# High and low weight parts kept in DRAM by the first token pass of a feed-forward stage and loaded by the second

## The chip, the cores and the metric

The kernel runs on one core of a Trainium2 chip. The metric is the device time of one execution in microseconds; the median of three runs is given for the kernel before, and a profiled execution has a span (first to last instruction) and a time of its own.

## What is computed

One layer of a diffusion backbone on 1,152 tokens (1,024 latent, 128 context) with 1,024 channels: adaptive RMSNorm, an input projection, three mixers, an output projection and a residual; then a second norm and a SwiGLU feed-forward stage, which is what matters here:

```python
h2 = _rmsnorm(x, p['norm2_g'][l]) * (1.0 + sc2) + sh2
f = (jax.nn.silu(h2 @ p['ffn_w1'][l]) * (h2 @ p['ffn_w3'][l])) @ p['ffn_w2'][l]
return x + g2 * f
```

`ffn_w1` and `ffn_w3` are 1024 x 2816, `ffn_w2` is 2816 x 1024, all fp32; a final RMSNorm follows.

## The kernel before

Each fp32 operand is split into a high part (a cast to fp32r, made by ScalarE, ACT) and a low part (the operand less its high part, a subtraction by GpSimd, POOL, or VectorE, DVE). `three` (lines 785 to 789) then makes a product with three matmuls, high by high, high by low and low by high, on TensorE (PE).

The feed-forward stage takes the tokens in two passes (`ph` 0 and 1): 640 tokens, then 512, in halves of 320 and 256 (`HN`). In each pass a loop runs over the 2816 hidden columns, in 22 tiles of 128, two tiles (f = 0, 1) to a pair: 11 pairs (`NFB`) per pass, numbered p = 0 to 21. For one tile, `up` (L1132) computes both h2 @ w1 and h2 @ w3 by a scheme of Strassen's kind: seven products (x = 0 to 6) of weight blocks of 512 rows by 128 columns instead of eight, 12 matmuls each. Four of the weight blocks are sums and differences of the quarters of [w1, w3]. `down` (L1164) multiplies the gated result of a pair with two tiles of w2 and adds it to `acc`.

For every tile of both passes:
- SyncE (SP) loads w1 and w3 columns into `raw13[f]` (`w13_in`, L522 to 527, two transfers of 512 KB with rows of 512 bytes) and, per pair, two tiles of w2 into `f2s` (`w2_in`, L529 to 533). SP issues in the order of its program and waits in that order.
- VectorE makes the four sums: `w_sum_13` (L2013, L2015) and `w_sum_24` (L2022, L2024).
- ScalarE makes seven high parts, 128x512 each, `w13_high` (L1523), into `w13h[x]`. There is one `w13h` buffer for each x, used by both tiles of a pair, so a new high part waits for the product x of the tile before.
- GpSimd makes the low parts of x = 0, 1, 3, 4, 6 (`w13_lo`, shown as L744) and VectorE those of x = 2 and 5 (L2029). They are written in place over the raw block or its sum.
- The low and high parts of w2 are made by `w2_lo` on GpSimd (L748) and `w2_high` on ScalarE (L1527).

The seven products go to four PSUM banks (`BANK_OF`), so block x=5 waits until VectorE has added up x=3 from bank 3 (`sum_3`, L2043), and x=6 and the next tile wait in the same way. VectorE's `sum_2` (L2037), `sum_3` (L2043, L2045, L2048), `gated_first`, `gated_second`, `f_low` (L2074) and `gather` (L2083) turn the products into the gated rows and add the down products to `acc`. ScalarE's `first_product`, `gate_a`, `gate_b` and `f_high` take part.

The order of the work on each engine is the order written out in `pair_first` (first tile of a pair) and `pair_second` (second tile and `down`), one pair of functions for ScalarE and one for VectorE; `pair_lows` is GpSimd's. In the second pass VectorE also does the end of the tokens already finished, one piece per pair (`early` and `late`): `gate_sum` (L2201) and `end_add` (L2205), 128x1024 additions, and `end_scale`; `early` stands ahead of `sum_2` of the second tile. SP loads the saved residual (`last_x2`, L558) and stores results (`result_out`, L563).

Of `up`, the waits of each block:

```python
if x == 4:
    pe.wait_ge(sem("gated_act"), cnt(6, pr, 3 * f + 1))
if x >= 5:
    pe.wait_ge(sem("combined"), cnt(18, pr, 9 * f + 2 * x - 8))
if x in POOL_LO:
    pe.wait_ge(sem("w13_lo"), cnt(10, pr, 5 * f + POOL_LO.index(x) + 1))
else:
    pe.wait_ge(sem("w13_lo_dve"), cnt(4, pr, 2 * f + DVE_LO.index(x) + 1))
```

Of the kernel before, what the change touches and what calls it, by code (L numbers as in the profile page):

```python
# [53 lines left out]
POOL_LO, DVE_LO = (0, 1, 3, 4, 6), (2, 5)  # L54
HID_POOL, HID_DVE = ((6,), (4, 6)), ((0, 1, 2, 3, 5, 4), (0, 2, 1, 3, 5))
# [35 lines left out]
def build(nc, A, O):  # L91
# [161 lines left out]
    def w13_low(x, f, dt=F32R):  # L253
# [32 lines left out]
    kb_dram = nc.dram_tensor("kb_dram", [32, NPAIR, 15 * HD], F32).ap()  # L286
    x2_dram = nc.dram_tensor("x2_dram", [T, D], F32).ap()
# [60 lines left out]
    def _(sp):  # L348
# [173 lines left out]
        def w13_in(pr, f, tile, first=False):  # L522

            if not first:
                sp.wait_ge(sem("product"), cnt(2 * NPR, pr, NPR * f - NPR))
            for e, w in enumerate(UP):
                sp.dma_start(raw13[f][:, e, :, :], A[w][0].rearrange("(k p) n -> p k n", p=P)[:, :, bass.ds(tile * P, P)]).then_inc(sem(f"x{3 + f}_in"), 16)
# [37 lines left out]
        def pair_in(ph, pr, tile, following, first=False):  # L565

            if not first:
                for f in range(FB):
                    w2_in(ph, pr, f, tile + f)
            w13_in((pr[0], pr[1] + 1), 0, following)  # L570
            w13_in((pr[0], pr[1] + 1), 1, following + 1)

        pair_in(0, (0, 0), 0, 2, True)
        with sp.Fori(1, NFB - 1) as it:
            pair_in(0, (it, 0), 2 * it, 2 * it + 2)
        pair_in(0, (0, NFB - 1), 2 * NFB - 2, 0)
        for p in range(NFB, 2 * NFB - 1):
            t = 2 * (p - NFB)
            pair_in(1, (0, p), t, t + 2)
# [12 lines left out]
        for f in range(FB):  # L592
            w2_in(1, (0, 2 * NFB - 1), f, 2 * NFB - 2 + f)
        for i in range(5, 8):
            result_out(i)
# [6 lines left out]
    def _(pool):  # L602
# [138 lines left out]
        def w13_lo(pr, f, x):  # L741
            pool.wait_ge(sem("w13_hi"), cnt(2 * NPR, pr, NPR * f + x + 1))
            pool.wait_ge(sem("w_sums"), cnt(8, pr, 4 * f + 4))
# [6 lines left out]
        def pair_lows(ph, pr, turn=False, last=False):  # L750

            after = (pr[0], pr[1] + 1)
            for x in POOL_LO:
                w13_lo(pr, 1, x)
            for f in range(FB):
                w2_lo(pr, f)
            if turn:
                for x in HID_POOL[1]:
                    hid_low(1, x)
            if not last:  # L760
                for x in POOL_LO:
                    w13_lo(after, 0, x)

        for x in (0, 1, 3, 4):
            w13_lo((0, 0), 0, x)
        hid_low(0, 6)
        w13_lo((0, 0), 0, 6)
# [24 lines left out]
    def _(pe):  # L792
# [339 lines left out]
        def up(ph, pr, f, first=False, turn=False, late=False):  # L1132

            n = HN[ph]
            for x in range(NPR):
# [11 lines left out]
                if x in POOL_LO:  # L1147
# [9 lines left out]
                wlo = w13_low(x, f)  # L1157
# [51 lines left out]
    def _(act):  # L1209
# [378 lines left out]
        for x in (0, 1):  # L1588
            w13_high(zero, 0, x, True)
# [3 lines left out]
        for x in (2, 3):  # L1593
            w13_high(zero, 0, x, True)
# [3 lines left out]
        for x in (4, 5):  # L1598
            w13_high(zero, 0, x, True)
        act.wait_ge(sem("o_done"), 2 * NT + 1)  # L1600
        w13_high(zero, 0, 6, True)
        h2_norm(NT - 1)
        gate_a(0, zero, 0)
        for x in range(6):
            w13_high(zero, 1, x)
# [4 lines left out]
        w13_high(zero, 1, 6)  # L1610
# [4 lines left out]
        def pair_first(ph, pr):  # L1615

            first_product(ph, pr, 0)
            for x in range(4):
                w13_high(pr, 1, x)
            gate_a(ph, pr, 0)  # L1620
            for x in (4, 5):
                w13_high(pr, 1, x)
            f_high(ph, pr, 0, 0)
            w13_high(pr, 1, 6)
# [3 lines left out]
        def pair_second(ph, pr, first=False, turn=False, last=False):  # L1628

            first_product(ph, pr, 1)  # L1630
            for f in range(FB):
                w2_high(ph, pr, f)
# [7 lines left out]
            if not last:  # L1640
                for x in range(NPR):
                    w13_high((pr[0], pr[1] + 1), 0, x)
# [44 lines left out]
    def _(dve):  # L1687
# [427 lines left out]
        w13_lo(zero, 0, 2)  # L2115
# [4 lines left out]
        w13_lo(zero, 0, 5)  # L2120
# [5 lines left out]
        w13_lo(zero, 1, 2)  # L2126
# [4 lines left out]
        w13_lo(zero, 1, 5)  # L2131
        f_low(0, zero, 0, 1)

        def pair_first(ph, pr, turn=False, late=False):

            if not late:
# [4 lines left out]
            if late:  # L2141
                w_sum_13(pr, 1)
                sum_3(ph, pr, 0)
            w_sum_24(pr, 1)
            if not late:
                sum_3(ph, pr, 0)
            w13_lo(pr, 1, 2)
# [3 lines left out]
            w13_lo(pr, 1, 5)  # L2151
            f_low(ph, pr, 0, 1)

        def pair_second(ph, pr, first=False, turn=False, early=None, late=None, gated=0):
# [19 lines left out]
            else:  # L2174
# [6 lines left out]
            if turn:  # L2181
                w_sum_13(after, 0)
                hid_low(1, 2)
            w_sum_24(after, 0)
            if late:
                late[0](late[1])
            for c in range(4, 2 * len(FT[ph])):
# [3 lines left out]
                if c == (7 if turn else 4):  # L2191
                    w13_lo(after, 0, 2)
                if c == 6 and not turn:
                    w13_lo(after, 0, 5)
            if turn:
                hid_low(1, 3)
                w13_lo(after, 0, 5)
# [35 lines left out]
        pair_first(1, (0, NFB), turn=True, late=True)  # L2233
# [11 lines left out]
        pair_first(1, last, late=True)  # L2245
# [93 lines left out]
```

## Time and profile before

| | |
|---|---|
| median of 3 runs | 1374.13 us (1367.06 to 1375.0) |
| profiled execution, its time | 1372.36 us |
| its span | 1370.5 us |
| PE busy | 1236.8 us (90%) |
| DVE busy | 1001.0 us (73%) |
| POOL busy | 645.8 us (47%) |
| ACT busy | 565.2 us (41%) |
| moved by DMA | 164.69 MB, 120 GB/s over the span |

The profile is of one execution. Busy is the time in which an engine had an instruction in flight; matmuls are pipelined and their ends are modelled, so PE's durations overlap. A row of a timeline gives start, duration, engine, line, what is written and read, and in brackets the idle time before and what ended it. The first pass runs from about 538 to 973 us of the span, the second from 973 to 1358; a pair begins where SP issues its `f2s` loads.

### The profile page before, as it was taken

The page shows a single profiled execution, that of the slowest core. Times are in us where ns is not written, and L with a number is a line of the kernel's source. Part 1 is how long each engine was busy: PE and PEld are TensorE (multiplying, and loading weights), DVE is VectorE, ACT ScalarE, POOL GpSimd, SP SyncE. Part 2 cuts the span into 40 slices and gives each one's busy share as a digit, 9 for nine tenths or more (in the row PEclk, how much of TensorE's full clock was granted, in tenths as well). Part 3 has the DMA queues.
Part 4 walks back from the last instruction along what each step waited for, and adds up shares of the span by engine and source line. Part 5 has one row for each costly group of instructions (what it writes and reads, how often), then busy time and mean ns, then how long its engine had stood idle before and what let it go on. Part 6 is the DMA issues. An engine that isn't in the chain of part 4 may idle for free.

```text
span 1370.5 us, 21592 instructions
## 1 busy us (share of the span) xinstructions
PE 1236.8 (90%) x7574; PEld 1089.7 (80%) x7574; DVE 1001.0 (73%) x1470; ACT 565.2 (41%) x1021; POOL 645.8 (47%) x426
## 2 busy tenths in 40 slices
PE   6786888995699999899999999999999999999986
PEld 4386787895446888799999999998788888888875
DVE  5437459949954347666667766667999899888988
ACT  2642531117245546543333333343443444344333
POOL 0495105275243003544554444544676666566662
PEclk9888998897799999999999999999999999999998
DMA  8814145379872323233223123222232333333331
GB/s 313 304 69 152 39 145 169 92 84 220 269 291 92 123 93 123 63 92 92 67 86 92 62 91 92 62 91 64 90 124 92 108 122 123 107 107 123 107 108 62
DMA packets 149089, 164.69 MB, mean 120 GB/s; under 512 B 7342, under 2 KB 124376, under 8 KB 146344
## 3 DMA queue, kind: packets, MB, share of 16 engines
q1 hardware_dynamic: 147664, 159.23, 37.5%
q0 software_dynamic: 1280, 4.72, 0.9%
q8 instruction: 30, 0.49, 0.1%
q14 instruction: 27, 0.22, 0.1%
q10 hardware_dynamic: 88, 0.02, 0.0%
HBM read 140.35 MB, written 23.59 MB: 120 GB/s over the span
## 4 chain that ended last, share of the span: by engine, by line
PE 62%; DVE 12%; issue 9%; ACT 6%; POOL 4%; DMA 4%; SPq 3%; DVEq 0%; ACTq 0%; POOLq 0%
PE banks L787 18%; PE banks L788 17%; PE banks L789 17%; PE banks L1056 2%; ACT w13h L1523 1%; DVE acc L2205 1%; DVE raw13r L2029 1%; DVE acc L2083 1%; DVE wsums L2022 1%; DMA ad<-in_ada_w 1%; PE banks L872 1%; SPq L483 1%; PE banks L823 1%; DMA y_dram<-yb 1%; SPq L425 1%
## 5 line engine op out<-in xcount | busy, mean ns | idle before, releaser
L744 POOL TENSOR_TENSOR raw13r<-raw13s,w13h 128x512 fp32r<-128x512 f32 x132 | 199.1, 1518 | 391.0 <-DVE wsums L2024 277.3
L788 PE MATMUL banks<-ntr,w13h 128*128 128x256 f32 (+1 forms) x1144 | 338.2, 296 | 0.0
L787 PE MATMUL banks<-ntr,w13h 128*128 128x256 f32 (+1 forms) x968 | 286.8, 296 | 32.9 <-DVE u L2043 25.2
L788 PEld LDWEIGHTS banks<-ntr,w13h 128*128 128x128 f32 x1144 | 217.3, 190 | 0.9
L787 PEld LDWEIGHTS banks<-ntr,w13h 128*128 128x128 f32 x968 | 184.2, 190 | 39.7 <-issue 29.5
L787 PE MATMUL banks<-f2h,f_hi 128*128 128x512 f32 x396 | 157.0, 397 | 2.4 <-DVE acc L2083 1.6
L788 PE MATMUL banks<-f2l,f_hi 128*128 128x512 f32 x396 | 156.5, 395 | 0.0
L789 PE MATMUL banks<-f2h,f_lo 128*128 128x512 f32 x396 | 156.3, 395 | 0.0
L789 PE MATMUL banks<-ntr,raw13r 128*128 128x256 f32 (+1 forms) x528 | 154.0, 292 | 0.0
L1523 ACT CAST w13h<-wsums 128x512 fp32r<-128x512 f32 x132 | 77.6, 618 | 169.9 <-DVE wsums L2022 162.1
L744 POOL TENSOR_TENSOR wsumr<-wsums,w13h 128x512 fp32r<-128x512 f32 x88 | 135.2, 1536 | 4.3 <-ACT w13h L1523 4.3
L748 POOL TENSOR_TENSOR f2l<-f2s,f2h 128x1024 fp32r<-128x1024 f32 x44 | 116.9, 2678 | 34.8 <-ACT f2h L1527 34.8
L789 PE MATMUL banks<-ntr,wsumr 128*128 128x256 f32 (+1 forms) x440 | 129.9, 295 | 0.0
L2083 DVE TENSOR_TENSOR acc<-acc,banks 128x512 f32<-128x512 f32 x170 | 111.7, 681 | 16.8 <-PE banks L789 14.1
L1523 ACT CAST w13h<-raw13s 128x512 fp32r<-128x512 f32 x176 | 101.8, 614 | 11.4 <-PE banks L789 11.4
L789 PEld LDWEIGHTS banks<-ntr,raw13r 128*128 128x128 f32 x528 | 100.0, 189 | 0.0
L787 PEld LDWEIGHTS banks<-f2h,f_hi 128*128 128x128 f32 x396 | 74.7, 189 | 21.1 <-DVE acc L2083 2.0
L789 PEld LDWEIGHTS banks<-f2h,f_lo 128*128 128x128 f32 x396 | 74.7, 189 | 17.6
L787 PE MATMUL banks<-nt_hi,w_hi 128*128 128x384 f32 x240 | 87.1, 363 | 1.6 <-DVE nt_lo L1804 1.6
L788 PEld LDWEIGHTS banks<-f2l,f_hi 128*128 128x128 f32 x396 | 74.7, 189 | 16.2
L787 PE MATMUL banks<-extr,w13h 128*128 128x320 f32 x264 | 82.0, 311 | 4.6 <-DVE u L2043 3.0
L788 PE MATMUL banks<-nt_lo,w_hi 128*128 128x384 f32 x240 | 85.0, 354 | 0.0
(321 smaller groups left out, 2764.7 us busy)
## 6 DMA issues: line engine op xcount, KB each, us to landing
raw13s<-in_ffn_w SPq DMA_DIRECT2D x88, 512.0 KB, 4.7
f2s<-in_ffn_w SPq DMA_DIRECT2D x44, 512.0 KB, 3.9
ad<-in_ada_w SPq DMA_DIRECT2D x20, 1024.0 KB, 10.0
wst<-in_w_in SPq DMA_DIRECT2D x10, 512.0 KB, 6.2
wc_dram<-wct POOLq DMA_DIRECT2D x16, 288.0 KB, 2.7
u<-z_dram SPq DMA_DIRECT2D x64, 72.0 KB, 3.2
kbw<-wc_dram SPq DMA_DIRECT2D x8, 576.0 KB, 6.1
wc<-wc_dram SPq DMA_DIRECT2D x16, 288.0 KB, 8.9
```

What stands on the lines that cost most here:

```text
L425: sp.dma_start(u8[i % 2][16 * s:16 * s + 16, :, :], dview(z_dram, i * P * CH * UC + s * UC, [[CH * UC, 16], [16 * CH * UC, 8], [1, UC]])). ...
L483: sp.dma_start(dview(y_dram, j * P * CH * UC + t * UC, [[CH * UC, 16], [16 * CH * UC, 8], [1, UC]]), yb[j % 2][16 * t:16 * t + 16, :, :]). ...
L744: nc.gpsimd.tensor_tensor(w13_low(x, f), w13_low(x, f, F32), w13h[x][:, :, :].bitcast(F32), ALU.subtract).then_inc(sem("w13_lo"), 1)
L748: nc.gpsimd.tensor_tensor(f2l[:, f, :], f2s[:, f, :], f2h[:, f, :].bitcast(F32), ALU.subtract).then_inc(sem("wo_lo"), 1)
L787: nc.tensor.matmul(out, hi_w, hi_x, start=start, stop=False)
L788: nc.tensor.matmul(out, hi_w, lo_x, start=False, stop=False)
L789: return nc.tensor.matmul(out, lo_w, hi_x, start=False, stop=stop)
L823: last = mm(bank[32 * q:32 * q + 32, :], condT[:, k, :], slot[:, 512 * q:512 * q + 512], start=(k == 0), stop=False)
L872: last = mm(B[n % 2][:, P * t:P * t + P], xt[i][:, P * k:P * k + P], diag[:, i, :], start=True, stop=True)
L1056: last = mm(B[5 + b][:, 0:n], wglu[:, k, P * m:P * m + P], yT[:, k, c0:c0 + n], start=(k == 0), stop=(k == 3))
L1523: nc.scalar.copy(w13h[x][:, :, :], w13_low(x, f, F32)).then_inc(sem("w13_hi"), 1)
L2083: TT(a, a, B[4 + c % 4][:, :], ALU.add).then_inc(sem("acc_done"), 1)
```

## The change

For five of the seven blocks (`KEPT`: x = 1, 2, 3, 5, 6) the first pass stores the high and the low part of every tile to a DRAM tensor `parts`, each 128 rows of 2 KB, and the second pass loads them instead of making them again. Blocks 0 and 4 (`RAW`) are quarters of w1; the second pass still loads w1 and splits these two. w3 is not loaded in the second pass, and its sums are not made there.

```diff
+KEPT, RAW = (1, 2, 3, 5, 6), (0, 4)
+PART = {1: ("w_in0_in", 128), 2: ("w_in1_in", 128), 3: ("w_part3", 0), 5: ("raws_in", 80), 6: ("w_part6", 0)}
+    w1b = at("w1b", [P, 4, P], O_WB + 28928, F32R)
+    parts = nc.dram_tensor("parts", [2 * NFB * 10 * P, 512], F32).ap()
...
+        def keep(pr, f, tile):
+            for x in KEPT:
+                if x in POOL_LO:
+                    sp.wait_ge(sem("w13_lo"), cnt(10, pr, 5 * f + POOL_LO.index(x) + 1))
+                else:
+                    sp.wait_ge(sem("w13_lo_dve"), cnt(4, pr, 2 * f + DVE_LO.index(x) + 1))
+                sp.dma_start(kept_at(tile, x, 0), flat(w13h[x][:, :, :])).then_inc(sem(PART[x][0]), 16)
+                sp.dma_start(kept_at(tile, x, 1), flat(w13_low(x, f))).then_inc(sem(PART[x][0]), 16)
+
+        def low_parts_in(p, f):
+            t = 2 * (p - NFB) + f
+            sp.wait_ge(sem("product"), 14 * p + 7 * f - 7)
...
+            sp.dma_start(raw13[f][:, 0, :, :], w1).then_inc(into, 16)
+            for x in (2, 3, 5, 6, 1):
...
+                sp.dma_start(flat(w13_low(x, f, F32R, 1)), kept_at(t, x, 1)).then_inc(into, 16)
+
+        def high_parts_in(p, f):
+            t = 2 * (p - NFB) + f
+            for x in KEPT:
+                sp.wait_ge(sem("product"), 14 * p + 7 * f - 7 + x + 1)
...
+                sp.dma_start(flat(w13h[x][:, :, :]), kept_at(t, x, 0)).then_inc(sem(PART[x][0]), 16)
...
+            keep(pr, 1, tile + 1)
+            w13_in((pr[0], pr[1] + 1), 0, tile + 2)
+            w13_in((pr[0], pr[1] + 1), 1, tile + 3)
+            keep((pr[0], pr[1] + 1), 0, tile + 2)
...
         for p in range(NFB, 2 * NFB - 1):
+            for f in range(FB):
+                w2_in(1, (0, p), f, 2 * (p - NFB) + f)
+            high_parts_in(p, 1)
+            low_parts_in(p + 1, 0)
+            high_parts_in(p + 1, 0)
+            low_parts_in(p + 1, 1)
```

On the engines: TensorE's block x in `KEPT` waits in the second pass for the transfer of its high part and for all six transfers of the tile's low parts and w1. GpSimd makes only x = 0 and 4 there. ScalarE casts only these two, and `w2_high` has moved from the second half of a pair to the first:

```diff
         def pair_first(ph, pr):
             first_product(ph, pr, 0)
-            for x in range(4):
-                w13_high(pr, 1, x)
+            if ph:
+                w13_high(1, pr, 1, 0)
+                for f in range(FB):
+                    w2_high(ph, pr, f)
+            else:
+                for x in range(4):
+                    w13_high(0, pr, 1, x)
```

VectorE makes in the second pass neither sums nor low parts; `sum_3` follows `sum_2` directly there. In the first pass ScalarE's cast into `w13h[x]` also waits until the tile before has been stored (for x in `KEPT`), `w_sum_24` until the low part of x=1 has, and SP's `w13_in` for the second tile until all low parts of that buffer have. Because the low part of x=1 has one buffer for both tiles, the second tile gets another one, `w1b`, in the second pass. SP's loop over the first pass is written out instead of a hardware loop. Blocks, matmuls, sums and their order in `up` and `down` are as before.

## Rows read from the trace of the kernel before

**Rows 1.** Stretches of one pair each: length, busy us (instructions), PE clock, DMA, GB/s.
```profile
core 0: us, PE busy (x) PEld busy (x) DVE busy (x) ACT busy (x) POOL busy (x), PEclk, DMA share, GB/s
735.60:774.10 38.50, 38.50 (x230) 35.87 (x229) 26.35 (x45) 13.86 (x26) 18.39 (x13) 1.00 0.27 82
...
973.40:1009.30 35.90, 34.21 (x226) 29.73 (x225) 31.17 (x47) 15.00 (x30) 19.95 (x12) 1.00 0.36 118
1009.30:1043.10 33.80, 31.60 (x218) 29.10 (x217) 30.57 (x45) 13.12 (x26) 22.17 (x13) 1.00 0.31 94
1043.10:1077.30 34.20, 31.69 (x218) 29.19 (x218) 30.78 (x45) 14.09 (x28) 22.33 (x13) 1.00 0.34 108
...
1146.20:1182.20 36.00, 33.16 (x218) 30.54 (x218) 31.44 (x46) 15.98 (x31) 21.91 (x13) 0.95 0.33 102
...
1319.70:1358.30 38.60, 34.31 (x216) 31.12 (x214) 35.23 (x44) 13.67 (x27) 23.88 (x13) 0.91 0.09 28
```

**Rows 2.** Who PE waited for, second pass: total us, times, longest.
```profile
PE banks L787 <- DVE u L2043: 25.2, 19, 2.2
PE banks L787 <- POOL raw13r L744: 3.4, 1, 3.4
PE banks L787 <- DVE xe L2256: 0.8, 1, 0.8
```

**Rows 3.** PE's timeline: start, duration; idle before and its releaser in brackets.
```profile
970.27 0.50 PE L787 MATMUL banks<-f2h,f_hi 128*128 128x512 f32 x1 [1.57 <-DVE acc L2083]
...
1063.00 0.38 PE L787 MATMUL banks<-ntr,w13h 128*128 128x256 f32 x1 [2.23 <-DVE u L2043]
1063.22 0.28 PE L788 MATMUL banks<-ntr,w13h 128*128 128x256 f32 x1
1063.34 0.28 PE L789 MATMUL banks<-ntr,raw13r 128*128 128x256 f32 x1
```

**Rows 4.** DVE's timeline around the same wait, and the next pair's L2201.
```profile
1056.22 1.78 DVE L2029 TENSOR_TENSOR raw13r<-raw13s,w13h 128x512 fp32r<-128x512 f32 x1
...
1058.26 3.41 DVE L2205 TENSOR_TENSOR acc<-acc,xe 128x1024 f32<-128x1024 f32 x1
...
1062.45 0.42 DVE L2043 TENSOR_TENSOR u<-u,banks 128x256 f32<-128x256 f32 x1
...
1073.66 1.22 DVE L2201 TENSOR_TENSOR acc<-acc,g2b 128x1024 f32<-128x1024 f32 x1
```

**Rows 5.** POOL's timeline at that time.
```profile
1058.04 5.86 POOL L748 TENSOR_TENSOR f2l<-f2s,f2h 128x1024 fp32r<-128x1024 f32 x2 [0.59 <-ACT f2h L1527]
```

**Rows 6.** One pair, instructions on raw13s alone (DVE, ACT, POOL), then on w13h.
```profile
1043.10:1077.30 34.20, 10.20 (x10) 4.63 (x8) 9.95 (x6) 1.00 0.34 108
...
1043.10:1077.30 34.20, 20.35 (x114) 17.30 (x113) 4.05 (x4) 7.87 (x14) 16.47 (x11) 1.00 0.34 108
```

**Rows 7.** Stretches with DMA queued: f2s, raw13s, 256 KB store, wc.
```profile
1045.00:1046.00 1.00, 1.00 (x11) 1.00 (x10) 0.97 (x2) 0.46 (x1) 1.00 (x2) 1.00 0.93 356
1057.00:1058.00 1.00, 1.00 (x10) 1.00 (x10) 1.00 (x2) 1.00 (x3) 0.45 (x1) 1.00 1.19 297
1367.00:1368.00 1.00, 0.00 (x0) 0.00 (x0) 0.68 (x2) 0.00 (x0) 0.00 (x0) 0.50 1.02 422
314.00:316.00 2.00, 0.00 (x0) 0.00 (x0) 1.97 (x2) 1.95 (x3) 1.90 (x2) 0.65 1.04 224
```

**Rows 8.** DMA issues of the page: count, size, median us from issue to landing.
```profile
f2s<-in_ffn_w SPq DMA_DIRECT2D x44, 512.0 KB, 3.9
```

**Rows 9.** Timelines of SP and DVE, first pass; an output's issue in the second.
```profile
747.89 13.27 SPq L527 DMA_DIRECT2D raw13s<-in_ffn_w  x4
...
750.07 0.68 DVE L2029 TENSOR_TENSOR raw13r<-raw13s,w13h 128x512 fp32r<-128x512 f32 x1
...
762.47 0.68 DVE L2013 TENSOR_TENSOR wsums<-raw13s 128x512 f32<-128x512 f32 x1
...
1110.45 0.36 SPq L563 DMA_DIRECT2D out<-acc  x1
```

More of the change, by code:

```diff
@@ L570, in pair_in @@
[L570 to L576, printed above, removed]
-        for p in range(NFB, 2 * NFB - 1):
-            t = 2 * (p - NFB)
-            pair_in(1, (0, p), t, t + 2)
+                    w2_in(0, pr, f, tile + f)
+            keep(pr, 1, tile + 1)
+            w13_in((pr[0], pr[1] + 1), 0, tile + 2)
@@ new lines, in pair_in @@
+            w13_in((pr[0], pr[1] + 1), 1, tile + 3)
+            keep((pr[0], pr[1] + 1), 0, tile + 2)
+        keep((0, 0), 0, 0)
+        pair_in((0, 0), 0, True)
+        for p in range(1, NFB - 1):
+            pair_in((0, p), 2 * p)
+        for f in range(FB):
+            w2_in(0, (0, NFB - 1), f, 2 * NFB - 2 + f)
+        keep((0, NFB - 1), 1, 2 * NFB - 1)
+        low_parts_in(NFB, 0)
+        high_parts_in(NFB, 0)
+        low_parts_in(NFB, 1)
+        for p in range(NFB, 2 * NFB - 1):
+            for f in range(FB):
[4 more added lines that the diff above has]
+            low_parts_in(p + 1, 1)
@@ L1630, in pair_second @@
             first_product(ph, pr, 1)
-            for f in range(FB):
-                w2_high(ph, pr, f)
+            if not ph:
+                for f in range(FB):
+                    w2_high(ph, pr, f)
             if turn:
@@ L2130, in _, with pair_first @@
         gated_second(0, zero, 0)
-        w13_lo(zero, 1, 5)
+        w13_lo(0, zero, 1, 5)
         f_low(0, zero, 0, 1)
-        def pair_first(ph, pr, turn=False, late=False):
-            if not late:
+        def pair_first(ph, pr, turn=False):
+            if not ph:
                 w_sum_13(pr, 1)
@@ L2140, in pair_first @@
                 hid_low(1, 5)
[L2141 to L2147, printed above, removed]
+            if not ph:
+                w_sum_24(pr, 1)
+            sum_3(ph, pr, 0)
+            if not ph:
+                w13_lo(0, pr, 1, 2)
             gated_first(ph, pr, 0)
@@ L2181, in pair_second @@
             if turn:
-                w_sum_13(after, 0)
                 hid_low(1, 2)
-            w_sum_24(after, 0)
+            elif not ph:
+                w_sum_24(after, 0)
             if late:
@@ L2190, in pair_second @@
                     hid_low(1, 1)
[L2191 to L2194, printed above, removed]
+                if c == 4 and not ph and not turn:
+                    w13_lo(0, after, 0, 2)
+                if c == 6 and not turn and not ph:
+                    w13_lo(0, after, 0, 5)
             if turn:
                 hid_low(1, 3)
-                w13_lo(after, 0, 5)
         def gate_sum(i):
@@ L2244, in _ @@
         last = (0, 2 * NFB - 1)
-        pair_first(1, last, late=True)
+        pair_first(1, last)
         def add_residual(i):
```

123 lines of the change are left out of this document (86 added, 37 removed).

## The prediction

> **What bounds the kernel now.** I read the table by stage first. A pair of weight tiles in the first token pass takes 38.5 us and TensorE is busy for all 38.5 of them; a pair of the second pass takes 34.2 us, with TensorE busy for 31.7 [rows 1]. The first pass is bound by the matmuls, and there only harm can be done. In the second pass about 2.5 us of each pair are waits, and VectorE (DVE) is busy for 30.8 of 34.2 us.
>
> The waits of TensorE over the second pass say who is late [rows 2]: 25.2 us in 19 waits for `u` L2043, the first addition of `sum_3`, which frees PSUM bank 3 for block x=5; 3.4 us in one wait for a low part that GpSimd (POOL) makes in the last pair; 0.8 us at the end. TensorE's timeline has a typical one, 2.23 us [rows 3], and VectorE's timeline says what L2043 was queued behind [rows 4]: a low part (L2029, 1.78 us), then `end_add` (L2205, 3.41 us), and only then `sum_2` and `sum_3`. An addition of the same size, L2201, takes 1.22 us at another moment [rows 4]. The slow one runs beside the `f2l` subtraction on GpSimd [rows 5], the fast one beside none. So the second pass is bound by VectorE's queue at one point per tile, and its additions get longer when GpSimd works.
>
> **What goes.** In the second pass all four sums and both low parts per tile leave VectorE: 10.2 us in ten instructions on the raw tiles [rows 6] and two low parts more on the summed ones, over a third of its 30.8 us per pair. ScalarE (ACT) loses 10 of 14 casts (7.87 us for 14, so 5.6 us), GpSimd 6 of 10 low parts (about 1.6 us each, so 10 us; the row counts one of a neighbouring pair too) [rows 6]. None of this is TensorE's time; it counts as far as waits vanish. The number of matmuls stays: a pair can't go below about 31.65 us, the busy time of most pairs [rows 1].
>
> To see which waits vanish I set T=0 at a pair's first matmul of the second pass. Matmuls follow each other by 0.12 us [rows 3], so a block (12 of them) is 1.43 us and a tile of seven 10.0 us; x=5 of the second tile is due at T = 10 + 7.15 = 17.15. The weights `f2s` land 3.9 us after their issue at T=0 [rows 8]. `w2_high` has moved to the first half of the pair: ScalarE makes its two casts between 4 and 6, ahead of `gate_a`, which can't start before block x=4 ends at 7.15 (if `f2s` came over 1 us late, `gate_a` would wait). So `f2l` (5.86 us for two [rows 5]) runs from about 5 to 11, and the low part of x=4 to 12.5. On VectorE, `gated_second` and the last `f_low` of the first tile end near 13; then `end_add` finds GpSimd idle, 1.22 us, to 14.2; `sum_2` to 14.7; block x=3 is done at 15.7, L2043 at 16.2: about 1 us before TensorE asks. If `end_add` still took 3.41 us, L2043 would end at 17.3 and the wait would be 0.2 us. In the first tile nothing stands between `sum_2` and `sum_3` any more, and L2043 ends at 6.2 for x=5 at 7.15. What is late next is that VectorE margin, not GpSimd: its last low part is ready at 12.5 and due at 15.7.
>
> The sum, against the profiled execution (span 1370.5 us, its time 1372.36; the median shown is 1374.13, 1.8 above, which the range takes in):
> - nine pairs from 1009.3 to 1319.7, where the last one starts [rows 1], 310.4 us, to 9 x 31.65 = 284.9: **-25.5**. In it are 1.5 us of one pair whose busy time is 33.16 at a granted clock of 0.95 [rows 1]: a stretch at the lower level (1.2 GHz) that follows a wait of 2 us.
> - the last pair, 38.6 us, to 31.65 + 0.8 for its end: **-6.1**. The 3.4 us wait goes, since GpSimd comes to its two residual additions, which stand ahead of the low part of x=0, without three low parts of the first tile; so does the clock (0.91) that fell after that wait [rows 1, 2].
> - the first pair of the second pass, 35.9 with 34.21 busy (it holds the gate rows) [rows 1]: **-1.7**; and the 1.57 us wait ahead of it for a gather [rows 3] that stands behind `w_sum_13`: **-1.6**.
>
> Together -34.9 at best. I give back 0.3 us per pair for the thin margin and for waits now on two semaphores per block, 11 x 0.3 = 3.3: **-31.6, so 1372.4 - 31.6 = about 1341 us.**
>
> **What is added: transfers.** In the first pass ten 262 KB stores per tile: with 2 MB of w1/w3 and 1 MB of w2 a pair moves 3.15 + 5.24 = 8.4 MB in 38.5 us, 218 GB/s. In the second, a tile loads w1 (0.52 MB) and ten 262 KB parts, a pair with w2 7.34 MB in 31.65 us, 232 GB/s, where before it was 94 to 118 [rows 1]. No such load is in the trace, so I bound its rate: 356 GB/s with 4 KB rows and 297 GB/s with 512 B rows while the queue is full, 422 GB/s for a 256 KB store with the very rows of the new ones, and as the lowest 224 GB/s, for the 288 KB `wc` pieces, at a share of 1.04 [rows 7]. The new pieces are contiguous and fill 128 partitions like the first three; `wc` fills 64. I take 340, nearest to those: 7.34 MB need 21.6 of 31.65 us, 8.4 MB need 24.7 of 38.5, both hidden behind matmuls. At 224 the second pass would take 32.8 us per pair: still under 34.2, but pairs that also move an `xe` or an output (0.52 MB each, about ten times) would lose 2.3 us each; that end is -34.9 + 11 x 1.12 + 10 x 2.34 = about +1, 1373.
>
> Timing matters beside rate, for SP issues in order. `high_parts_in(p,1)` waits block by block behind `w2_in`; each part is issued when the first tile's block x ends and due 6 blocks = 8.6 us later. Ahead of it is at most 1 MB of `f2s`, 3.9 us to landing [rows 8]. `low_parts_in` is issued at T = 10 and 20 and due at 31.65 and 41.65. `result_out`, which waits for VectorE's `end_scale`, stands behind these in a pair and ahead of the next `w2_in`; it was issued at 1110.45 [rows 9], 1.1 us before its pair ended, and VectorE is not later now. SP issues 24 transfers per pair instead of 6, at 0.36 us [rows 9] 8.6 us of 31.65. So I cost the order at nothing; the cover is 4.7 us for the high parts, and each us beyond is a us of every pair.
>
> In the first pass the new waits: `keep(pr,1)` stands ahead of `w13_in` on SP and waits for the last low part, VectorE's (750.07 + 0.68), so SP's load moves from 747.89 to about 752; behind up to 0.5 MB of stores it lands near 758 (two 0.52 MB transfers, as `f2s`, plus the stores' 1.5 us), and its first reader, L2013, starts at 762.47 [rows 9]. Cover: 4 us; gone, each us beyond costs at most one per pair. `keep(pr+1,0)` delays `w2_in` by about 2 us; its reader `w2_high` stands behind the whole first tile there. ScalarE's new wait for the stored high part and `w_sum_24`'s for the low part of x=1 come a tile after those stores. Nothing.
>
> At this place the Trainium skill speaks against the change: DMA: Bandwidth & Descriptors, section Measured, fits one transfer as 2.0 us plus its bytes by 436 GB/s and wants transfers of 1 MiB. By that fit, as an estimate, a 256 KB piece costs 2.6 us and a pair's 20 pieces and 4 larger ones 65 us, if each waited for the one before; by it the time would be that of rival D. The trace has pieces of this size with the engines at a share of 1.04 [rows 7]: they overlap.
>
> **Rivals.**
> A, only half the waits go. If `end_add` and `gate_sum` still hold VectorE too long in the second tile (2.2 us x 9, and the 1.5 us of clock behind one), the gain is 34.9 - 21.3 = 13.6: **1359**. For it: VectorE's slow additions last as long as GpSimd's instruction beside them [rows 4, 5], and my margin is 1 us. Against: the low part ahead of `end_add`, 1.78 us, is gone, and `f2l` has moved.
> B, hidden anyway or eaten up: transfers near 224 GB/s, worked out above: **1373**.
> C, the other side: the transfers become the bound. It decides at 7.34 MB / 34.2 us = 215 GB/s in the second pass and 218 in the first. At 200 the ten first-pass pairs take 42 us (+35) and the second pass (11 x 7.34 + 5.2 MB) 430 instead of 385 (+45): **1452**; at 210, +15 and +24, **1411**. For it: the `wc` row lies 3% above that bound, and reads and writes of DRAM now mix. Against: three rows with 128 partitions at 297 to 422.
> D, that pieces run one at a time: with half of `f2s`'s 3.9 us [rows 8] for a piece of half its size, 20 pieces and four of 3.9 us are 55 us per pair, 21 above the 34.2 of now: **1600**. The full share in [rows 7] speaks against it.
>
> **How the numbers follow.** Forecast (1330 to 1350) 0.64; A (1350 to 1362) 0.15; B 0.08; C 0.10; D 0.03. The forecast and A hold 0.79, so the range is 1330 to 1362. A measurement of this kernel tells about 1% from no change, 1360.4 to 1387.9. Faster: the forecast and nearly all of A, 0.78. Same: B and the rest of A, 0.10. Slower: C, D, less the mildest of C, 0.12.
>
> **What would show it.** Pairs of the first pass still 38.5 us, at 200 to 225 GB/s. Pairs of the second pass 31.6 to 32.2 us, VectorE busy for under 20 us of them, GpSimd about 12. The row "PE banks <- DVE u" shrinks from 25.2 us to under 4; no TensorE wait on `w13h`'s DMA. `end_add` at 1.2 us confirms the margin, at 3.4 it is A. DMA share in the second pass 0.65 to 0.75; near 1.0 it is B or C. The prediction is wrong if block x=1 to 3 of the second tile waits for its DMA, or if a pair of the first pass grows.

## The result, and the profile after

| | before | after |
|---|---|---|
| median | 1372.59 us (4 runs, 1367.06 to 1375.0) | 1325.15 us (4 runs, 1323.28 to 1326.07) |
| span of the profiled execution | 1370.5 us | 1323.8 us |

The ratio is 0.9658, with a 95% interval of 0.9625 to 0.9691: 47 us faster. 31.6 were forecast (to 1341, with a range of 1330 to 1362), so the direction was right and the size was not.

The table by stage, pair by pair as in [rows 1] (length, busy us of each engine with its instructions, granted clock, DMA share, GB/s):

```profile
732.00:770.90 38.90, 38.90 (x233) 36.26 (x232) 26.79 (x45) 14.05 (x27) 18.43 (x12) 1.00 0.64 219
...
925.00:966.40 41.40, 38.38 (x217) 35.48 (x216) 34.09 (x43) 17.82 (x28) 20.79 (x11) 0.96 0.64 226
966.40:999.60 33.20, 33.20 (x226) 29.73 (x226) 17.53 (x33) 10.19 (x20) 10.19 (x6) 1.00 0.77 254
1061.80:1092.90 31.10, 31.10 (x218) 29.00 (x218) 17.07 (x34) 12.04 (x21) 10.09 (x6) 1.00 0.81 270
1248.40:1280.40 32.00, 31.64 (x218) 28.83 (x218) 17.33 (x34) 8.13 (x16) 10.06 (x6) 1.00 0.80 280
1280.40:1311.60 31.20, 31.20 (x216) 28.52 (x215) 23.06 (x37) 11.46 (x22) 12.38 (x6) 1.00 0.24 76
```

The first pass is as long as it was: nine pairs took 346.7 us before and 346.9 now, with 219 GB/s where there were 82. In the second pass eight of the nine pairs take 31.1 us with TensorE busy for all of them; VectorE works 17 to 18 us in a pair instead of 30.8, GpSimd 10 instead of 22. One pair keeps a wait of 0.4 us and takes 32.0. TensorE's waits from 940 us on (total, times, longest), which answer to [rows 2]:

```profile
PE banks L862 <- DVE u L2143: 3.0, 1, 3.0
PE banks L862 <- DVE acc L2317: 0.4, 1, 0.4
```

The 3.0 us stand at the end of the first pass, where the kernel before has them too. Of the 25.2 us of waits for `sum_3` in the second pass nothing is left. VectorE's timeline in the pair that begins at 1061.81, which answers to [rows 4]:

```profile
1073.94 1.22 DVE L2303 TENSOR_TENSOR acc<-acc,xe 128x1024 f32<-128x1024 f32 x1
1075.42 0.42 DVE L2137 TENSOR_TENSOR u<-xs,banks 128x256 f32<-128x256 f32 x1 [0.26 <-DVE acc L2303]
1077.49 0.42 DVE L2143 TENSOR_TENSOR u<-u,banks 128x256 f32<-128x256 f32 x1 [1.66 <-PE banks L864]
```

And of TensorE, the pair's first matmul (T = 0) and the first of block x=5 of the second tile:

```profile
1061.62 0.28 PE L862 MATMUL banks<-ntr,w13h 128*128 128x256 f32 x1
...
1078.71 0.28 PE L862 MATMUL banks<-ntr,w13h 128*128 128x256 f32 x1
```

`end_add` takes 1.22 us, and `sum_3` now waits for TensorE, not TensorE for it: its first addition ends at 1077.91, T = 16.29, and block x=5 starts at T = 17.09. The margin is 0.80 us; the prediction had 16.2, 17.15 and about 1. The DMA part of the page (count, size, median us to landing), beside [rows 8]:

```profile
parts<-w13h SPq DMA_DIRECT2D x110, 256.0 KB, 2.4
w13h<-parts SPq DMA_DIRECT2D x110, 256.0 KB, 2.7
f2s<-in_ffn_w SPq DMA_DIRECT2D x44, 512.0 KB, 4.2
...
wsumr<-parts SPq DMA_DIRECT2D x55, 256.0 KB, 4.9
```

**Where 46.7 us of span went.** Three landmarks, the same in both traces: the start of the 3.02 us wait at the end of the first pass (949.15 and 944.10), the starts of the pairs, and the last pair's end.

| stretch | before | after | difference | forecast |
|---|---|---|---|---|
| up to the wait at the first pass's end | 949.15 | 944.10 | -5.1 | 0 |
| from there to the second pass | 24.2 | 22.3 | -1.9 | -1.6 |
| its first pair | 35.9 | 33.2 | -2.7 | -1.7 |
| nine pairs | 310.4 | 280.8 | -29.6 | -25.5 |
| last pair | 38.6 | 31.2 | -7.4 | -6.1 |
| given back for new waits | | | 0 | +3.3 |

The first row needs a closer look, for the change touches nothing up to 530 us. VectorE's first `sum_2` marks the start of the feed-forward stage. Of before, of after, and of the third experiment below, which has the same code up to there as after:

```profile
539.83 0.47 DVE L2037 TENSOR_TENSOR u<-xs,banks 128x320 f32<-128x320 f32 x1
```
```profile
534.64 0.47 DVE L2137 TENSOR_TENSOR u<-xs,banks 128x320 f32<-128x320 f32 x1
```
```profile
527.57 0.47 DVE L2133 TENSOR_TENSOR u<-xs,banks 128x320 f32<-128x320 f32 x1
```

In the eleven kernels profiled here, with the same work up to this point, it starts between 527.57 and 539.83, and before's execution is the latest of all. The six kernels with the code of before up to there are spread from 530.12 to 539.83, the five with that of after from 527.57 to 537.05. The granted clock of an early stretch goes roughly with it; the stretch 220 to 260 us of before, and of the third experiment:

```profile
220.00:260.00 40.00, 34.75 (x221) 30.50 (x221) 39.10 (x60) 5.02 (x10) 9.02 (x7) 0.84 0.42 131
```
```profile
220.00:260.00 40.00, 35.83 (x265) 31.97 (x260) 39.14 (x60) 8.01 (x14) 13.59 (x9) 1.00 0.46 144
```

So 5 of the 46.7 us between the two profiles are not the change's but the executions'. Counted from the first `sum_2` to the end of the span, which leaves this out, before takes 830.7 us and after 789.2: the change is worth 41.5. Whether the 47 us between the two medians hold the same 5 is not shown, for one execution of each kernel is traced; the runs of before taken beside the experiments have medians of 1371.0, 1371.1 and 1367.4, which lie 42 to 46 us above after's. The experiments are given in both measures.

| kernel | median, us | first `sum_2` to end, us | nine pairs, us |
|---|---|---|---|
| before | 1372.6 | 830.7 | 310.4 |
| after | 1325.2 | 789.2 | 280.8 |
| e1 VectorE relieved | 1331.0 | 790.5 | 281.3 |
| e2 GpSimd relieved | 1334.1 | 795.1 | 281.3 |
| e3 w2 split late | 1324.6 | 790.6 | 280.8 |
| e4 end work behind | 1346.0 | 812.0 | 290.5 |
| e5 more transfers | 1327.4 | 790.0 | 280.8 |
| e6 turn, w2 early | 1327.2 | 788.4 | 280.8 |
| e7 f2l in quarters | 1351.8 | 812.1 | 293.8 |
| e8 turn, all | 1322.7 | 786.5 | 280.8 |
| e9 order and quarters | 1344.6 | 807.2 | 288.9 |

### The profile page after: what moved, and what is told of

It reads as the page before. It is cut to its first block, busy times and chain, and to the rows that moved or that the text cites. A ratio compares the mean times of both kernels' runs of the same rounds, so it can differ in the third digit from the quotient of the medians.

```text
span 1323.8 us, 21436 instructions
## 1 busy us (share of the span) xinstructions
PE 1220.8 (92%) x7574; PEld 1080.5 (82%) x7574; DVE 850.8 (64%) x1338; ACT 511.0 (39%) x911; POOL 516.0 (39%) x360
## 4 chain that ended last, share of the span: by engine, by line
PE 76%; DMA 5%; issue 4%; POOL 4%; ACT 4%; DVE 3%; SPq 3%; DVEq 0%; ACTq 0%; POOLq 0%
PE banks L862 22%; PE banks L864 22%; PE banks L863 22%; PE banks L1131 3%; DMA ad<-in_ada_w 1%; PE banks L898 1%; PE banks L947 1%; SPq L436 1%; ACT nts L1660 1%; PE banks L1013 1%; POOL psum_w L751 1%; POOL sst L791 1%; DMA z_dram<-zp 1%; POOL pu L757 1%; PE banks L1136 1%
## 5 line engine op out<-in xcount | busy, mean ns | idle before, releaser
L814 POOL TENSOR_TENSOR raw13r<-raw13s,w13h 128x512 fp32r<-128x512 f32 x110 | 155.1, 1418 | 467.1 <-ACT w13h L1612 421.9
L863 PE MATMUL banks<-ntr,w13h 128*128 128x256 f32 (+1 forms) x1144 | 336.1, 294 | 0.0
L862 PE MATMUL banks<-ntr,w13h 128*128 128x256 f32 (+1 forms) x968 | 282.5, 292 | 4.4 <-ACT xs L1622 2.3
L2183 DVE TENSOR_TENSOR acc<-acc,banks 128x512 f32<-128x512 f32 x170 | 112.7, 684 | 38.9 <-PE banks L864 30.8
L818 POOL TENSOR_TENSOR f2l<-f2s,f2h 128x1024 fp32r<-128x1024 f32 x44 | 106.1, 2432 | 34.1 <-ACT f2h L1616 34.1
L864 PE MATMUL banks<-ntr,wsumr 128*128 128x256 f32 (+1 forms) x396 | 116.3, 294 | 0.0
L863 PEld LDWEIGHTS banks<-f2l,f_hi 128*128 128x128 f32 x396 | 74.6, 188 | 16.2
L2042 DVE SCALAR_TENSOR_TENSOR banks<-vp,pv,banks 128x1167 f32<-128x1167 f32 x58 | 83.4, 1438 | 2.0
L864 PE MATMUL banks<-nt_hi,w_lo 128*128 128x384 f32 x240 | 83.5, 348 | 0.0
L1612 ACT CAST w13h<-raw13s 128x512 fp32r<-128x512 f32 x132 | 77.1, 614 | 11.4 <-PE banks L864 11.4
```

Of the source, the lines that this page charges most:

```text
L814: nc.gpsimd.tensor_tensor(w13_low(x, f), w13_low(x, f, F32), w13h[x][:, :, :].bitcast(F32), ALU.subtract).then_inc(sem("w13_lo"), 1)
L818: nc.gpsimd.tensor_tensor(f2l[:, f, :], f2s[:, f, :], f2h[:, f, :].bitcast(F32), ALU.subtract).then_inc(sem("wo_lo"), 1)
L862: nc.tensor.matmul(out, hi_w, hi_x, start=start, stop=False)
L863: nc.tensor.matmul(out, hi_w, lo_x, start=False, stop=False)
L864: return nc.tensor.matmul(out, lo_w, hi_x, start=False, stop=stop)
L1612: nc.scalar.copy(w13h[x][:, :, :], w13_low(x, f, F32)).then_inc(sem("w13_hi"), 1)
```

## The experiments

**e1: VectorE relieved, nothing stored or loaded.** To the kernel before (`second` is true in the second pass; `w_sum_24` and VectorE's `w13_lo` return alike):

```diff
         def w_sum_13(pr, f):
+            if second(pr):
+                return
...
-                wlo = w13_low(x, f)
+                wlo = w13h[x] if ph and x in (2, 5) else w13_low(x, f)
```

> The kernel before, in which VectorE makes no weight sums and no low parts in the second pass (they are left out: ScalarE casts whatever the buffers hold, and the low operand of blocks x=2 and x=5 is the high part). Nothing is stored or loaded more, and GpSimd keeps its ten low parts per pair. Theory 1 (VectorE's queue ahead of sum_3 held TensorE, and a pair without waits takes 31.1 us): the nine pairs that took 310.4 us take 280 to 285, no wait at sum_3 over 0.3 us, the time falls by 27 to 35 us, to 1338 to 1346. Theory 2 (the pair's floor is the 31.65 us of the busy time): the same without waits, but 285 to 289 for the nine. Rival (GpSimd's low parts were as late as VectorE, and the additions beside them stay at 3.4 us): waits of 1 us or more stay, 1352 to 1362.

Measured 1331.0 us, ratio 0.9723 (0.9685 to 0.9761). One of its pairs, and all of TensorE's waits from 950 us on:

```profile
1033.20:1064.30 31.10, 31.10 (x218) 29.00 (x218) 19.50 (x33) 16.06 (x30) 18.60 (x12) 1.00 0.37 118
```
```profile
PE banks L794 <- DVE acc L2235: 0.7, 1, 0.7
PE banks L794 <- DVE xe L2272: 0.7, 1, 0.7
```

Theory 1 holds and theory 2 falls: the pair takes 31.1 us at the DMA load of before, so this floor lay in the kernel before already. GpSimd still made its ten low parts (for them it no longer waits for VectorE's sums), and none was late, not even the one of the last pair [rows 2]: what VectorE lost is enough for the whole gain of the second pass. The time fell by more than the 27 to 35 us expected, by 40.2 from the first `sum_2` on.

**e2: GpSimd relieved.** To the kernel before:

```diff
-            for x in POOL_LO:
+            for x in (0, 4) if ph else POOL_LO:
                 w13_lo(pr, 1, x)
```

> The kernel before, in which GpSimd makes only the low parts of x=0 and x=4 in the second pass (six of ten per pair are left out: the low operand of x=1, 3 and 6 is the high part). VectorE keeps its sums and low parts, and the f2l subtraction stays where it was. Theory (the wait is VectorE's queue at one point, and the one GpSimd instruction beside end_add is f2l): end_add stays at about 3.4 us, the nine pairs keep their waits of about 2 us (300 to 311 us together), the last pair loses its 3.4 us wait and 2 us of clock behind it; 1362 to 1370. Rival (GpSimd's work as such slows VectorE all over the pair): VectorE's busy time per pair falls by 3 us or more, the waits go, 1340 to 1350.

Measured 1334.1 us, ratio 0.9738 (0.9693 to 0.9783). The theory failed and the rival holds, with a time 6 us under the rival's: VectorE has all its work, is busy 5 to 6 us less in a pair, and TensorE no longer waits in the nine pairs. One of them:

```profile
1033.10:1064.30 31.20, 31.20 (x218) 29.01 (x218) 24.65 (x45) 14.26 (x28) 11.46 (x7) 1.00 0.37 118
```

The groups of VectorE instructions by line, from 1010 to 1300 us (count, busy us, mean ns), first of before, then of e2:

```profile
L2029 DVE TENSOR_TENSOR raw13r<-raw13s,w13h 128x512 fp32r<-128x512 f32 x18 | 22.1, 1228 | 0.0
L2015 DVE TENSOR_TENSOR raw13s<-raw13s 128x512 f32<-128x512 f32 x17 | 20.5, 1205 | 0.6
L2205 DVE TENSOR_TENSOR acc<-acc,xe 128x1024 f32<-128x1024 f32 x5 | 17.1, 3414 | 0.0
```
```profile
L2026 DVE TENSOR_TENSOR raw13s<-raw13s 128x512 f32<-128x512 f32 x18 | 14.5, 807 | 0.6
L2040 DVE TENSOR_TENSOR raw13r<-raw13s,w13h 128x512 fp32r<-128x512 f32 x19 | 13.0, 682 | 0.0
L2216 DVE TENSOR_TENSOR acc<-acc,xe 128x1024 f32<-128x1024 f32 x6 | 7.3, 1220 | 0.0
```

The same low part takes 682 ns instead of 1228. Taking work from GpSimd made VectorE faster all over the pair, end_add included, though `f2l` is still there: `end_add` now comes before it.

**e3: the split of w2 back in the second half.** To the kernel after:

```diff
-            if not ph:
-                for f in range(FB):
-                    w2_high(ph, pr, f)
+            for f in range(FB):
+                w2_high(ph, pr, f)
```

> The changed kernel with the casts of w2 (f2h) back in the second half of a pair, behind first_product, and with GpSimd's low part of x=4 ahead of f2l again. Theory (with the sums and low parts gone from VectorE, sum_3 has a margin of 1 to 2 us, so the slow addition is affordable): end_add goes from 1.22 back to about 3.4 us, waits at sum_3 of at most 0.3 us in the pairs that have an end_add, 0 to 5 us above the changed kernel, 1325 to 1330. Rival (moving w2's split is what freed sum_3): waits of 1.5 to 2.2 us in seven to nine pairs, 1338 to 1348.

Measured 1324.6 us, ratio 0.9683 (0.9632 to 0.9733), and 790.6 us from the first `sum_2`: no difference that can be told. There is no cost where up to 5 us were expected, and the reason given was not the right one: `end_add` stays short (lines of 1010 to 1300 us), since VectorE comes to it before `f2l` starts (in one pair at 1067.11, `f2l` at 1068.04).

```profile
L2299 DVE TENSOR_TENSOR acc<-acc,xe 128x1024 f32<-128x1024 f32 x6 | 7.3, 1218 | 0.0
```

Moving w2's split, on which the prediction spent a paragraph, was not what freed `sum_3`.

**e4: one reordering, no work removed.** To the kernel before:

```diff
-            if early:
-                early[0](early[1])
             sum_2(ph, pr, 1)
...
             sum_3(ph, pr, 1)
+            if early:
+                early[0](early[1])
```

> The kernel before with one reordering on VectorE: the end's work of a pair (end_add, gate_sum, end_scale) stands behind sum_3 of the second tile, not ahead of sum_2. All work stays, no transfers are added. Theory (the order at one point, not the amount): the 2.2 us waits at the first addition of sum_3 go; end_add now stands ahead of gated_first, so f_low of the second tile comes later and its readers in the down projection wait 0 to 1.5 us; 1345 to 1362. If no wait is left, a pair of the nine takes 31.1 us with all the work still in it, which would show the floor without the change. Rival (VectorE's load per pair is the bound): the same 2 us of wait turn up at another place, 1366 to 1374.

Measured 1346.0 us, ratio 0.9837 (0.9788 to 0.9885). One pair, and TensorE's largest waits from 950 us on:

```profile
1096.30:1128.70 32.40, 31.36 (x218) 29.06 (x217) 29.75 (x46) 16.83 (x32) 21.99 (x13) 1.00 0.40 129
```
```profile
PE banks L787 <- DVE u L2043: 9.5, 11, 1.6
PE banks L787 <- POOL raw13r L744: 3.4, 1, 3.4
```

The theory holds as to the second tile, and `f_low` is not late. What is left, up to 1.04 us in a pair, is `sum_3` of the first tile, behind `w_sum_13` and `w_sum_24` there: for that part the sums had to go. VectorE's timeline beside GpSimd's shows how one kind of addition can take two durations:

```profile
1114.40 1.22 DVE L2205 TENSOR_TENSOR acc<-acc,xe 128x1024 f32<-128x1024 f32 x1
...
1116.69 1.48 DVE L2062 TENSOR_TENSOR fv<-fv,xs 128x256 f32<-128x256 f32 x1
...
1111.92 5.96 POOL L748 TENSOR_TENSOR f2l<-f2s,f2h 128x1024 fp32r<-128x1024 f32 x2 [0.58 <-ACT f2h L1527]
```

`f2l` is two instructions. In after, where VectorE's instructions beside them read PSUM (all but the last, which starts 0.1 us before they end), the two take 4.76 us, 2.38 each:

```profile
1066.23 4.76 POOL L818 TENSOR_TENSOR f2l<-f2s,f2h 128x1024 fp32r<-128x1024 f32 x2 [0.72 <-ACT f2h L1616]
```

In e4 the first would then end at 1114.30. `end_add` starts at 1114.40, is not slowed at all, and the second `f2l` ends about 1.22 us later than it would have: 4.76 + 1.22 = 5.98, and the row has 5.96. The multiplication at 1116.69, 0.42 us of work at other times, ends 0.3 us after that. In the kernel before, `end_add` starts 0.2 us after the first `f2l` has begun. If it stands until that one is done, at 1060.42, and works 1.22 us, it ends at 1061.64; the trace has 1061.67 [rows 4, 5]. So the 3.41 us are a turn that had to be waited for, not slow work.

The Trainium skill, SBUF — State Buffer, section Who interferes with whom, says so: a VectorE instruction with two SBUF inputs and a GpSimd instruction that reads SBUF exclude each other, and whichever comes second stands still until the first is done. These rows agree, and so does `acc<-acc,banks`, with one input in PSUM: 682 ns in before, 687 in after.

**e7: f2l in quarters.** That reading says that the wait is one GpSimd instruction long. To the kernel before:

```diff
+            n = D // parts
+            for q in range(parts - 1):
+                h = slice(q * n, q * n + n)
+                nc.gpsimd.tensor_tensor(f2l[:, f, h], f2s[:, f, h], f2h[:, f, h].bitcast(F32), ALU.subtract)
...
-                w2_lo(pr, f)
+                w2_lo(pr, f, 4 if ph else 1)
```

> The kernel before, in which GpSimd makes each f2l subtraction of the second pass in four instructions of 256 columns and not in one of 1024. Nothing else changes. Theory (the port is held for one GpSimd instruction at a time: end_add's 3.41 us are 2.2 us of standing still behind one f2l instruction and 1.22 of work): end_add takes 1.3 to 2.0 us, the 2.2 us waits of TensorE at sum_3 fall to about 1, the pairs of 34.2 us to 32.5 to 33.3; 1355 to 1363. Rival (VectorE and GpSimd share the port, each slower as long as both work): end_add stays above 3 us, 1368 to 1374.

Measured 1351.8 us, ratio 0.9875 (0.9843 to 0.9908). `end_add` by line, and TensorE's wait from 920 us on, 3.0 of it at the turn of the passes:

```profile
L2210 DVE TENSOR_TENSOR acc<-acc,xe 128x1024 f32<-128x1024 f32 x6 | 10.6, 1758 | 0.0
```
```profile
PE banks L792 <- DVE u L2048: 14.0, 20, 3.0
```

1.76 us is 1.22 and about one quarter (2.38 / 4 = 0.60). The rival, both slower as long as both work, falls. The nine pairs gain 16.6 us together: about 1.65 us each, which is what `end_add` gains (in three of the pairs other end work stands in its place), and 1.5 us more in the one pair that had the lowered clock [rows 1], for no pair has it here. The median is 3 us under what was expected, no more than the executions differ by.

**e9: order and quarters together**, the edits of e4 and e7.

> The kernel before with two edits of order alone: end_add and the other end work behind sum_3 (1346 us by itself) and f2l in quarters (1352 by itself). No work is taken away and nothing is stored or loaded more. Theory (a wait at one point of VectorE's queue, made of instructions that stand still behind GpSimd's): waits at sum_3 of 0 to 0.5 us, the nine pairs at 31.1 to 31.8, 1340 to 1346; the last pair keeps its 3.4 us wait for GpSimd and the first one its gather. Rival (the two edits act on the same 2 us): no better than the first alone, 1345 to 1349.

Measured 1344.6 us, ratio 0.9838 (0.9807 to 0.9868), 4.8 us below e4 from the first `sum_2` on. The medians don't tell it from e4, and five of the nine pairs still take 32.3 to 32.6 us: neither the theory nor the rival holds as it was put. TensorE's wait for `sum_3` of the first tile is there as in e4 (0.98 us in the pair at 1126.7). Order and shorter instructions, with all work kept and no transfers added, give 23.5 of the change's 41.5 us; the rest came, in e1 and e2, with less work on VectorE or GpSimd. Whether another order would give it was not tried.

**e5: more transfers.** To the kernel after:

```diff
+                r = t * 10 * P + 2 * KEPT.index(x) * P
+                sp.dma_start(again[r:r + P, :], parts[r:r + P, :]).then_inc(sem("again"), 16)
```

> The changed kernel with one transfer more behind each high part of the second pass: the same 262 KB are copied from the buffer in DRAM to another place in DRAM, which nobody reads: ten a pair, 2.6 MB on top of 7.3 to 8.4, on the same queue. Theory (the transfers of the change are covered with room): the changed kernel's pairs move 237 to 280 GB/s at a share of 0.71 to 0.81, so the full share would be worth about 335 to 345 GB/s, and the pairs now need 320 to 365: the pairs without other transfers stay at 31.1 us, the fuller ones grow by up to 2.5 us; 1325 to 1345. Rival (the change was already close to the transfers' limit, rival C of the prediction): every pair waits for its parts, 34 us or more, 1360 and above.

Measured 1327.4 us, ratio 0.9702 (0.9658 to 0.9745). Two of its pairs, and where its parts land:

```profile
1093.20:1124.30 31.10, 31.10 (x219) 28.99 (x218) 18.98 (x34) 11.97 (x21) 10.02 (x6) 1.00 0.97 355
...
1217.60:1248.70 31.10, 31.10 (x219) 29.00 (x218) 18.07 (x34) 9.34 (x17) 10.03 (x6) 1.00 1.00 355
```
```profile
w13h<-parts SPq DMA_DIRECT2D x110, 256.0 KB, 4.6
again<-parts SPq DMA_DIRECT2D x110, 256.0 KB, 5.1
```

The high parts land 1.9 us later than in after, within the cover of 4.7 us that the prediction named, and no pair waits for a transfer: 31.1 us at 355 GB/s and a share of 1.00. (One wait of 0.3 us for `sum_3` is new in the last pair.) The theory holds, with more room than expected.

**e6 and e8: the turn of the passes.** The largest wait left is the 3.0 us at 944.10. The additions in front of it, of after:

```profile
940.25 3.03 DVE L2091 TENSOR_TENSOR nts<-nts 128x1024 f32<-128x1024 f32 x1
943.20 3.39 DVE L2104 TENSOR_TENSOR ntr<-nts,ntr 128x1024 fp32r<-128x1024 f32 x1
```

They are beside `f2l` again. e6, to the kernel after, in the last pair of the first pass alone: `w2_high` behind the casts of x=0 to 3 in `pair_first`, GpSimd's `w2_lo` behind three of its five low parts.

> The changed kernel with w2's casts and the f2l subtraction of the last pair of the first pass moved to that pair's first half, as the change did in the second pass. Theory (a VectorE addition with both inputs in SBUF that starts while a GpSimd instruction runs stands still until that one ends, and 1.22 us of work follow): hid_sum(1,1) and hid_low(1,0), 3.03 and 3.39 us beside f2l, take 1.22 us each, L2143 comes in time, the 3.02 us wait of TensorE at the turn goes and the lowered clock behind it (0.55 and 0.88 of 3 us each) with it: 4 to 5 us less, 1319 to 1322. Rival (the wait at the turn is that of a chain from ScalarE's casts of the hidden state, whatever GpSimd does): no change, 1324 to 1326.

Measured 1327.2 us, ratio 0.9686 (0.9661 to 0.9711). Its rows of the same two additions, of TensorE at `sum_3`, and the 3 us behind the wait:

```profile
936.73 1.21 DVE L2097 TENSOR_TENSOR nts<-nts 128x1024 f32<-128x1024 f32 x1
937.86 1.21 DVE L2110 TENSOR_TENSOR ntr<-nts,ntr 128x1024 fp32r<-128x1024 f32 x1
```
```profile
939.60 0.41 PE L865 MATMUL banks<-extr,w13h 128*128 128x320 f32 x1 [1.94 <-DVE u L2149]
```
```profile
941.00:944.00 3.00, 3.00 (x13) 3.00 (x12) 1.91 (x4) 0.93 (x2) 0.00 (x0) 0.50 1.00 372
```

The two additions are short, as expected, but TensorE's wait falls by 1.1 us only: VectorE comes to `sum_2` 1.3 us ahead of the time at which TensorE asks for `sum_3`, where it was 4.3 in after, because an `f_low` (2.08 us) now stands behind the earlier `f2l` and a low part (1.77) behind one of GpSimd's low parts. The turn had moved along the same queue. And behind a wait of 1.94 us the clock was still at the lower level, 1.2 GHz (0.50). The pair went from 41.4 to 40.4 us, and the time from the first `sum_2` on fell by 0.8 us, not by the 4 to 5 expected. e8 moves the two additions as well (to the kernel of e6):

```diff
             sum_2(ph, pr, 1)
+            sum_3(ph, pr, 1)
             if turn:
                 hid_sum(1, 1)
-                hid_low(1, 0)
-            sum_3(ph, pr, 1)
-            if turn:
                 hid_sum(1, 2)
...
             f_low(ph, pr, 1, 1)
             if turn:
+                hid_low(1, 0)
```

> The run before last (the changed kernel with w2's casts and f2l early in the last pair of the first pass) with VectorE's turn reordered too: hid_sum(1,1) stands behind sum_3 and hid_low(1,0) behind the two f_low. With f2l early those two took 1.21 us each, but TensorE still waited 1.94 us at sum_3 and its clock still fell to 0.50 behind that wait; this pair took 40.4 us, 41.4 in the changed kernel. Theory (what stands ahead of sum_3 is the whole of it): no wait over 0.3 us in that pair, no lowered clock, 37 to 38 us for the pair, and about 1320 to 1323 for the whole, which the spread of the runs (1318 to 1334) may hide. Rival (hid_low(1,0), later now, is what the next tile waits for, or f_low is late): a wait of 1 to 3 us at the next tile's first block or in the down projection, the pair at 40 us or the next one longer by as much.

Measured 1322.7 us, ratio 0.9661 (0.9630 to 0.9691). The pair, and TensorE's one wait in it:

```profile
928.00:966.00 38.00, 37.15 (x217) 33.79 (x217) 33.23 (x43) 17.79 (x28) 21.27 (x11) 1.00 0.68 247
```
```profile
PE banks L865 <- DVE acc L2189: 0.8, 1, 0.8
```

38.0 us at a full clock, and no wait for `sum_3`: the theory holds in the main. But where no wait above 0.3 us was expected, TensorE waits 0.85 us for a gather ahead of the down products, the place that the rival named. By the traces e8 is 2.7 us ahead of after (786.5 against 789.2); the medians can't tell them apart.

## Why the prediction was right and wrong

**What bounds the kernel: right.** The second pass was held by VectorE's queue ahead of `sum_3`; e1 reaches the floor by relieving VectorE alone, and the change's checkpoints are met: no wait there, `end_add` at 1.2 us, a margin of 0.8 us for the 1 foreseen, VectorE under 20 us in each of the nine pairs. Rival A falls, for half of the waits would have had to stay and none did.

**The floor: wrong, 4.1 us in the nine pairs, and 0.5 of the 1.3 in the last.** The step that failed is "a pair can't go below about 31.65 us, the busy time of most pairs". The true floor is 31.1, and e1 shows it without the change's transfers. A pair's busy time goes with its waits: 31.7 at 2.5 us of wait [rows 1], 31.36 at 1.04 (e4), 31.10 at none. TensorE's timeline of before, ahead of the wait in [rows 3], and two matmuls of the down projection, say why:

```profile
1060.38 0.28 PE L788 MATMUL banks<-ntr,w13h 128*128 128x256 f32 x1
1060.49 0.28 PE L789 MATMUL banks<-ntr,raw13r 128*128 128x256 f32 x1
...
1066.42 0.39 PE L789 MATMUL banks<-f2h,f_lo 128*128 128x512 f32 x1
1066.65 0.39 PE L787 MATMUL banks<-f2h,f_hi 128*128 128x512 f32 x1
```

Matmuls follow each other by 0.12 us but each counts as busy for 0.28, and after a wait the second one follows by 0.22. From 1060.49 to 1063.22 two steps of 0.12 take 2.73: 2.49 are lost, and the trace calls 2.23 of them idle. Each wait hides 0.26 us, two a pair 0.5. The floor follows from the steps, not from the busy time: a pair has 168 matmuls of `up` at 0.119 and 48 of `down` at 0.232 (medians over the second pass of before), 20.0 + 11.1 = 31.1 us. At that floor the nine pairs' term would have been 310.4 - 279.9 = 30.5, and 29.6 came. The Trainium skill, Perfetto Trace Analysis, section Tensor Engine Instruction, says that the end of a matmul in a trace is estimated, not observed; these rows agree, and the prediction took the busy time all the same.

**The give-back: wrong, 3.3 us.** The 0.3 us a pair for a thin margin and double waits were set without a row, and the pairs show nothing of the kind: busy time equals length in eight of nine.

**The smaller terms: right in kind.** The last pair gave 7.4 for 6.1, the first pair 2.7 for 1.7, the gather 1.9 for 1.6. In the last pair the 0.8 us set aside for its end, a wait for `xe` [rows 2], did not come; in the first, 0.26 of the 1.0 is what its one wait hid, and the rest is open. The reason given for the last pair, GpSimd's three low parts of the first tile, is not the only one: in e1 GpSimd keeps them, and the 3.4 us wait is gone as well.

**The execution: 5.1 us that no step could hold.** The sum was made against one execution whose feed-forward stage began at 539.83, the latest of eleven. Against another one the forecast would have been lower by up to 12. By the change's 41.5 us alone the time would have come to 1331. The three errors, 4.1 + 1.3 + 1.0 + 0.3 of the terms, 3.3 and 5.1, make the 15.1 us between -31.6 and the -46.7 of the spans.

**Transfers: right.** Rivals B, C and D all fall: 237 to 280 GB/s in the second pass and 219 in the first, hidden, and e5 puts the bound of the second at 355 or more. The estimate of 340 was near, on the low side; the 224 of the 64-partition `wc` did not bind here. The 20 pieces overlap: a store of the high parts lands in 2.4 us, and yet 24 transfers fit into 31.1 us. By the fit of the Trainium skill, DMA: Bandwidth & Descriptors (it stands in section Anatomy of one DMA — SWDGE (gpsimd) path, not in Measured, and is made for transfers that GpSimd issues), one piece takes 2.6 us, as an estimate; for one piece the trace agrees, though SP issues it. The prediction's 65 us for a pair at that price do not give rival D's 1600, as it says: 11 pairs, each 31 us above 34.2, are 1711.

**Why VectorE was slow: half seen.** The prediction said that its additions get longer beside GpSimd, and that the fast L2201 at 1073.66 [rows 4] ran beside nothing. GpSimd had work then, but began it 0.17 us later, and it was GpSimd's low part that took longer, 2.21 us where the same part takes 1.29 in after:

```profile
1073.83 2.21 POOL L744 TENSOR_TENSOR raw13r<-raw13s,w13h 128x512 fp32r<-128x512 f32 x1 [9.93 <-DVE wsums L2024]
```

They take turns, so where VectorE reads both inputs from SBUF, what GpSimd does is VectorE's time. The prediction counted work by engine; e2 came as a surprise for the same reason.

## What to carry to other kernels

Take the floor of a stage that TensorE bounds from the steps between matmuls times their number, not from its busy time, which counts part of each wait. Where a VectorE addition with both inputs in SBUF has two durations, look at what GpSimd runs when it starts: shorter GpSimd instructions, another order, or less work on either of the two gives the time back, before any transfers are bought for it. e1 and e2 leave out work that the result needs, so they show where the time lies and are no kernels to use; e4, e7 and e9 leave out nothing. And compare two profiles from a landmark behind which the code differs: here 12 us of spread lie ahead of it.

## What the hardware showed that was not expected

VectorE and GpSimd took turns by whole instructions: 1.22 us of addition took 3.41 behind one `f2l` instruction, 1.76 behind a quarter of one, and 1.22 between two. Transfers of 256 KB held 355 GB/s at a DMA share of 1.00 through a stage in which TensorE never waited. TensorE's granted clock fell to 0.50 behind a wait of 1.94 us at the turn of the passes, and stayed at 1.00 in that pair when 0.85 us was the longest. No rule follows from that: in the second pass of before nine pairs have a wait of 1.9 to 2.2 us, and one of them a lowered clock (0.95 over the pair [rows 1]).
